# All eight residual additions behind a post-norm on VectorE, in order, instead of four on VectorE and four on GpSimd

## What is computed

```python
h = h + rms_norm(m, mix_post_g[layer])
f = squared_relu_mlp(rms_norm(h, ffn_pre_g[layer]), w_ff1[layer], w_ff2[layer])
h = h + rms_norm(f, ffn_post_g[layer])
```

## Time and profile before

| | us |
|---|---|
| median of 3 runs | 2329.52 |
| lowest and highest run | 2323.38, 2329.62 |
| span of the profiled execution | 2327.8 |

### The profile page before, as it was taken

One profiled execution on the slowest core, in us unless ns is written; L12 is line 12 of the kernel. 1 busy time (PEld: TensorE's weight loads), 2 busy tenths in 40 slices (PEclk: granted clock), 3 DMA queues, 4 the chain that ended last, 5 costly groups with the idle time before them and its releaser, 6 DMA issues.

```text
span 2327.8 us, 23709 instructions
## 1 busy us (share of the span) xinstructions
PE 2109.0 (91%) x9104; PEld 1646.9 (71%) x9104; DVE 878.8 (38%) x1221; ACT 776.6 (33%) x1059; POOL 787.5 (34%) x231
## 2 busy tenths in 40 slices
PE   7764789999998899899999897888989988999999
PEld 5442558888876667588888675567877776888887
DVE  3999332112115352411111225676532122524333
ACT  5432443213224353323223336462113223213221
POOL 4664124444433311344444421030002432434433
PEclk9887889999998999899999998997879999999999
DMA  4110122232220121132232211010001222232232
GB/s 159 54 36 0 55 82 91 90 101 97 91 90 14 63 73 37 36 109 90 92 106 91 90 64 55 19 64 10 1 1 54 95 86 73 91 108 91 90 104 77
DMA packets 28009, 164.78 MB, mean 71 GB/s; under 512 B 3451, under 2 KB 5788, under 8 KB 10524
## 3 DMA queue, kind: packets, MB, share of 16 engines
q1 hardware_dynamic: 27932, 163.71, 20.4%
HBM read 160.03 MB, written 3.67 MB: 70 GB/s over the span
## 4 chain that ended last, share of the span: by engine, by line
PE 77%; DVE 10%; issue 7%; ACT 4%; POOL 1%; DMA 0%; DVEq 0%; ACTq 0%; SPq 0%; POOLq 0%
PE ps L1351 63%; PE ps L1310 4%; DVE Z L1123 2%; DVE NT L914 1%; PE ps L1668 1%; DVE Y L914 1%; POOL wlo L379 1%; ACT whi L433 1%; PE ps L1495 1%; PE ps L1657 1%; PE ps L1483 1%; PE ps L1666 1%; PE ps L1512 1%; PE ps L1513 1%; PE ps L1608 1%
## 5 line engine op out<-in xcount | busy, mean ns | idle before, releaser
L379 POOL TENSOR_TENSOR wlo<-wraw,whi 128x2048 fp32r<-128x2048 f32 (+4 forms) x163 | 687.4, 4218 | 1396.6 <-ACT whi L433 1396.6
L1351 PE MATMUL ps<-xh,whi 128*128 128x512 f32 x1436 | 577.2, 402 | 43.7 <-DVE xl L846 27.0
L1351 PE MATMUL ps<-xl,whi 128*128 128x512 f32 x1436 | 567.2, 395 | 0.0
L1351 PE MATMUL ps<-xh,wlo 128*128 128x512 f32 x1436 | 566.8, 395 | 0.0
L433 ACT ACTIVATE whi<-wraw 128x2048 fp32r<-128x2048 f32 (+4 forms) x163 | 285.0, 1748 | 387.5 <-PE ps L1351 385.3
L1351 PE MATMUL ps<-hh,whi 128*128 128x512 f32 x904 | 359.6, 398 | 9.1 <-DVE hl L948 5.0
L1351 PEld LDWEIGHTS ps<-xh,whi 128*128 128x128 f32 x1436 | 275.1, 192 | 113.2 <-issue 29.5
L1351 PE MATMUL ps<-hl,whi 128*128 128x512 f32 x904 | 353.5, 391 | 0.0
L1351 PE MATMUL ps<-hh,wlo 128*128 128x512 f32 x904 | 353.3, 391 | 0.0
L1351 PEld LDWEIGHTS ps<-xl,whi 128*128 128x128 f32 x1436 | 275.2, 192 | 61.0 <-issue 4.3
L1351 PEld LDWEIGHTS ps<-xh,wlo 128*128 128x128 f32 x1436 | 274.6, 191 | 58.4
(11 more groups left out here) (228 smaller groups left out, 1982.2 us busy)
## 6 DMA issues: line engine op xcount, KB each, us to landing
wraw<-stream SPq DMA_DIRECT2D x136, 1024.0 KB, 4.9
wraw<-stream SPq DMA_DIRECT2D x8, 512.0 KB, 3.6
wraw<-stream SPq DMA_DIRECT2D x4, 768.0 KB, 4.3
wraw<-stream SPq DMA_DIRECT2D x6, 384.0 KB, 3.1
resid<-x SPq DMA_DIRECT2D x4, 512.0 KB, 5.4
wraw<-stream SPq DMA_DIRECT2D x8, 256.0 KB, 3.0
out<-resid SPq DMA_DIRECT2D x4, 512.0 KB, 2.6
E<-rel_scratch SPq DMA_DIRECT2D x8, 128.0 KB, 4.2
```

The lines of the kernel that those rows point to most:

```text
L379: pool.tensor_tensor(wlo[:, p, 0:w], wraw[:, p, 0:w], whi[:, p, 0:w], ALU.subtract).then_inc(lo_ready, 1)
L1351: ins = pe.matmul(ps[:, 2 * p + n, :], wt[:, p, w], xt[:, k0 + k, :], start=k == 0 and q == 0, stop=k == k_tiles - 1 and q == 2)
```

## The change

VectorE does all eight additions. Behind the multiplication of tile j (from tile 1 on) it adds tile j - 1, and tile 7 comes last. GpSimd has no additions any more and its loops over the chunks are no longer broken there. One semaphore, `resid_ready`, counts all eight tiles, and what waited for two semaphores waits for one.

```diff
-RES = {n: DT // 2 * i for i, n in enumerate(("mix0", "ffn0", "mix1", "ffn1"))}
+RES = {n: DT * i for i, n in enumerate(("mix0", "ffn0", "mix1", "ffn1"))}
...
         def resid_at(eng, name):
-            return lambda j: eng.wait_ge(resid_odd_ready if j % 2 else resid_ready, RES[name] + j // 2 + 1)
+            return lambda j: eng.wait_ge(resid_ready, RES[name] + j + 1)

         def resid_all(eng, name):
-            for j in (DT - 2, DT - 1):
-                resid_at(eng, name)(j)
+            resid_at(eng, name)(DT - 1)
...
-            adds = {START["ffn_0"] + 1: "mix0_post", START["latent"] + 1: "ffn0_post",
-                    START["ffn_1"] + 1: "mix1_post", START["sq"] + 1: "ffn1_post"}
-            for c, n in runs(DT + 2, N_CHUNK, adds):
-                if c in adds:
-                    for j in range(1, DT, 2):
-                        pool.wait_ge(root_read, READS0[adds[c]] + j + 1)
-                        pool.tensor_tensor(resid[:, j, :], resid[:, j, :], Y[:, j, :],
-                                           ALU.add).then_inc(resid_odd_ready, 1)
+            for c, n in runs(DT + 2, N_CHUNK):
...
                     dve.scalar_tensor_tensor(out=Y[:, j, :], in0=Y[:, j, :], scalar=gain(j), in1=ps[:, ROOT, :],
                                              op0=ALU.mult, op1=ALU.mult).then_inc(root_read, 1)
-                    if j % 2:
+                    if j:
                         add(j - 1)
+                add(DT - 1)
```

More of the change, by code:

```diff
@@ L241, in build @@
         dve_step, act_step = sem("dve_step"), sem("act_step")
-        resid_ready, resid_odd_ready = sem("resid_ready"), sem("resid_odd_ready")
+        resid_ready = sem("resid_ready")
         squares_ready, squares_summed = sem("squares_ready"), sem("squares_summed")
```

## The result

The changed kernel takes 2332.91 us in the median (5 runs, 2329.22 to 2336.45), the kernel before 2325.22 us (5 runs, 2323.09 to 2329.62). The ratio is 1.0033 with a 95% interval of 1.0021 to 1.0044: it is slower by about 7.7 us, which is a little over the 0.3% that a measurement of this kernel can tell. A second measurement gave 1.0030 (1.0019 to 1.0041).

A forecast was written before the change was run, and what follows sets the result against it. TensorE was taken as the bound, 77% of the chain, with its sums deciding at the places. Three places at 0.25 plus 0 elsewhere gave 0.8 us, span 2328.6, median 2330.3; range 2323.5 to 2336.5.

The forecast's parts named there:

- VectorE's own additions, cost 0: At each of three places, add 7 ends at 708.7 instead of 707.36, hidden by TensorE's low-clock sums: cost 0.
- The hold-up, 2.12 us: At each place GpSimd's earlier `rest` holds the shared SBUF port, so VectorE's add 0 ends 2.12 us later.
- The clock's rise keeps its place: During TensorE's sums, the rise stays at 707.28, 3.87 behind sum 0; 1.2 of 2.12 us is caught up.
- The next product gives back 0.45 or more: TensorE's product behind the sums starts 0.9 later but loses slow time, so a place costs 0.45 to -0.1.
- falls only later: In the gap before the next product, a later clock fall lets 1.2 us run fast; place costs about -0.1.
- Behind the convolution, cost 0: Add 0 is caught there too, but ScalarE's table copies cover it by 2.6 and 3.9 us: cost 0.
- 0.2 to 0.3 a place: Net cost in us at each of three places, the middle between two cases for the next product's clock.
- A: At three places the clock's rise moves along with sum 0, delay stays whole: 6.4 us, 2335.9; chance 0.15.
- B: At three places the low-clock stretch becomes 3.4 us longer: 10.2 us slower in all, 2339.7; chance 0.11.
- D: At the places add 0 isn't held up and nothing changes: 2329.5; chance 0.08 shared with another no-change case.
- E: GpSimd's slower additions, 1.65 against 0.68, might let places win, yet 0 expected; chance 0.08 shared with another no-change case.
- C: The clock stays up through the gap before the next product: -1.9 us a place, 2323.8; chance 0.10.

The follow-up runs named there:

- the products in PSUM: Changed kernel, with the multiplication by gain and root writing into PSUM so each addition has one SBUF input; ratio to the kernel before 1.0009 (1.0000 to 1.0017).
- `rest` held at the three places: Changed kernel, GpSimd's rest of the second chunk waiting for all eight additions everywhere but behind the convolution; ratio to the kernel before 1.0004 (0.9996 to 1.0013).
- the one with `rest` held: Changed kernel, GpSimd's rest of the second chunk waiting for all eight additions at all four places; ratio to the kernel before 1.0003 (0.9994 to 1.0012).
- eight fills: Kernel before with eight scratch-tile fills on VectorE ahead of tile 0's multiplication at three places, a plain delay; ratio to the kernel before 1.0069 (1.0056 to 1.0082).

## Why the prediction was right in kind and too small

- **VectorE's own additions, cost 0.** Right: 1.0003 with only them, and the place at 13.32 us. The condition named with it held too: with the sums at the high clock they cost 1.54 us a place.
- **The hold-up, 2.12 us.** Right: sum 0 starts 4.82 us behind the multiplication of tile 0 instead of 2.82, 2.0 later. `rest` started 0.16 behind the rounding, add 0 took 2.70 us, and the multiplications weren't stopped.
- **The clock's rise keeps its place.** Right at two places, wrong at the third. Behind feed-forward 0 it came 3.9 to 4.0 us behind sum 0 (forecast 3.87) and the root 1.02 late (forecast 0.9); behind feed-forward 1 4.2 and 1.16. Behind the attention it came 5.3 behind, and the root 1.99 late. I had worked one place out and taken three alike. But the way from place 1 to place 2 is not the same length in two executions, so the phase in which place 2 is met isn't either. How much that does without any hold-up two experiments show: with the products in PSUM, and with `rest` held at the three places, the clock rose 4.1 and 4.0 us behind sum 0 at place 2 instead of 5.9 (at 951.61 and 950.64), and the place took 12.40 and 12.36 us instead of 13.28. So the 1.99 of one place is no fixed price of the hold-up.
- **The next product gives back 0.45 or more.** This step failed at place 1, at least for the first 20.8 us. The case "falls only later" did occur there (low stretch 3.4 us instead of 6.8), and won nothing. From the first rounding of the split to the copy of the first latent product it takes 20.78 us in the changed kernel (first fence below, 713.72 to 734.50) and the same 20.78 in the kernel before with matmuls of constants (second fence, 709.46 to 730.24), in which no low stretch lies at this place. In the kernel before it is 20.79. ScalarE's copy stands behind its sixteen roundings, and what TensorE does faster isn't seen. By the dividing instruction at 879 the changed kernel is 0.6 and 0.7 us ahead of the first profile of the kernel before (167.01 and 166.87 against 167.59) and 0.4 and 0.6 ahead of the one with `rest` held (167.44), so some of it may come back later on. Behind the attention 0.87 came back, behind feed-forward 1 0.1. The same 364.71 us behind the attention stand in the two experiments just named, so the 0.87 goes with the short low stretch there (3.4 us in all of them, 6.8 in the kernel before) and not with the hold-up.

```profile
713.72 1.29 ACT L464 ACTIVATE xh<-NT 128x512 fp32r<-128x512 f32 x2 [0.82 <-DVE NT L843]
...
734.50 1.01 ACT L567 ACTIVATE E<-ps 128x1024 f32<-128x1024 f32 x1
```

```profile
709.46 0.63 ACT L472 ACTIVATE xh<-NT 128x512 fp32r<-128x512 f32 x1 [0.81 <-DVE NT L851]
...
730.24 1.01 ACT L575 ACTIVATE E<-ps 128x1024 f32<-128x1024 f32 x1
```

- **Behind the convolution, cost 0.** Right: 17.98 and 17.99 us, and 1.0004 with the hold-up there alone.
- **The sum.** The mis-sized term is "0.2 to 0.3 a place". In the profiles the three places cost 4.2 us less 0.9 and 0.1, thus 3.2 instead of 0.8. That the two profiled spans differ by 3.0 is an accident: the changed kernel took 1.0 us more between place 1 and place 2 and 1.2 less ahead of place 1.
- **What the sum left out.** The medians differ by 7.0 to 7.7 us, not 3. The profiled execution of the kernel before was a long one (2329.52 us against a median of 2325.22); its second profile is 5.9 us shorter, 3.36 of them between place 1 and place 2. In the mean of two profiles each, the spans differ by 6.7 us: 3.4 at the places and behind places 2 and 3, 2.6 between place 1 and place 2 (232.56 and 235.92 against 236.79 and 236.89), and 0.8 ahead of place 1, all rounded. I had given low stretches elsewhere a chance of 0.06 and no price. Of the 2.6 us, 1.6 are the passage near 890, and there the two kernels differ in every profile. The other 1.0, and the 0.8, are less than what the two profiles of the kernel before differ by at the same spots (3.4 and 2.3 us), so they may be the luck of four executions. Why the passage near 890 has its low stretch in the changed kernel stays open.
- **The rivals.** A (nothing given back, +6.4) gave nearly the measured total, but not for its reason: at two places 1 us was given back. B's longer low stretch wasn't seen in the changed kernel. It was with eight fills, where 10.2 us stood in place of 6.8 at place 1 (700.6 to 710.8). D fell with the 2.70 us. E fell too: even without the hold-up VectorE's quicker additions won nothing (1.0003 with `rest` held, 1.0009 with the products in PSUM). C didn't come about: the clock fell in the gap behind each of the three places.

## A faster version

The kernel before with four matmuls of constants ahead of the sums and four behind them at three places takes 2309.9 us, ratio 0.9937 (0.9921 to 0.9954), some 15 us less than the kernel before. It keeps the split of the additions, which under a high clock is worth 1.5 us a place.

## What to carry to other kernels

Before an instruction is taken out of an engine's queue, look at what it held back, and what that will now meet: here four additions on GpSimd kept a 4.5 us instruction away from VectorE's additions. If GpSimd holds up a VectorE instruction with two SBUF inputs, as here, moving one of them to PSUM can cure it without any order of the queues. A delay ahead of work that runs at a low clock is partly given back and partly carried into low stretches elsewhere, so price it at each place by that place's own waits, and by more than one profile.

## What the runs showed of the hardware that was not expected

- Executions of one program differed by 3.36 us over the same 233 us of instructions, with the granted clock 0.89 in one and 1.00 in the other over 15 us of it, and by 2.3 us in the 698 us ahead of them; in the 1380 us behind they agreed to 0.2 us.
- An idle time of 0.46 us on VectorE stood 3.1 us behind the same instruction in all seven profiles in which VectorE had eight additions more ahead of it, and 4.7 us behind it in the five in which it had none more.
- A delay of 5.13 us at three places, 15.4 us in all, cost 16 us (13 to 19 by the interval), one of 2.49 us at the same places (7.5 in all) 4.9 us (2.1 to 7.4).
- Eight extra matmuls a place, 24 in all, made the kernel 15 us faster; ten more in two other gaps made no difference.
